# An attention and RWKV decoder layer on one core: ranking by eight-largest operations, the compression's first rows and weights loaded one stage earlier, and the dilated cache's loads issued from three queues

## What is computed

```
P = h @ w_in                               # one projection, split among all branches
A = native sparse attention:
      compressed blocks: each block of 32 cached rows (stride 16) of keys and of values goes through
                         hid = gelu((rows + phi_pe) @ phi_w1); row = hid @ phi_w2
      selected blocks:   score of each of 65 blocks of 64 tokens from the compressed weights, plus a bonus
                         for forced blocks; the 16 highest (ties: lower index first) are attended in full
      window:            the last 512 tokens
B = RWKV-7 time mixing (a recurrence)
C = dilated window attention, 3 groups of 4 heads with (window, step) = (128,1), (512,4), (2048,16)
m = sum of the three branches, gated;  x = LayerNorm(alpha * x + gate * (m @ w_o))
x = LayerNorm(alpha * x + gate * SwiGLU(x))
```

## Time and profile before

| | us |
|---|---|
| median of 3 runs | 2117.22 |
| runs | 2113.62 to 2125.13 |
| the profiled execution | 2136.6 |
| its span, first to last instruction | 2134.8 |
| TensorE busy | 1816.2 (85%) |
| VectorE busy | 1066.3 (50%) |
| ScalarE busy | 667.8 (31%) |
| GpSimd busy | 201.3 (9%) |
| mean granted TensorE clock | 0.919 of full speed |

### The profile page before, as it was taken

One profiled execution on the slowest core, in us unless ns is written; L12 is line 12 of the kernel. 1 busy time (PEld: TensorE's weight loads), 2 busy tenths in 40 slices (PEclk: granted clock), 3 DMA queues, 4 the chain that ended last, 5 costly groups with the idle time before them and its releaser, 6 DMA issues. The chain is left out here.

```text
span 2134.8 us, 39918 instructions
## 1 busy us (share of the span) xinstructions
PE 1816.2 (85%) x16882; PEld 1633.4 (77%) x16882; DVE 1066.3 (50%) x1722; ACT 667.8 (31%) x1306; POOL 201.3 (9%) x245
## 2 busy tenths in 40 slices
PE   3898788887989869998877999656599799999996
PEld 1898678776888868897875667434499699999996
DVE  3114656666655325685865545592276443333333
ACT  1225333332212212332324766323342422221122
POOL 0000000000001114221100001244100000000000
PEclk7999899998999988999987999778799899999998
DMA  6546754342536758766656252657363133232221
GB/s 245 152 123 199 208 154 142 112 152 90 172 111 202 225 163 273 194 204 174 147 145 259 88 154 66 199 175 260 119 225 112 30 99 90 81 90 82 83 72 43
DMA packets 334304, 315.61 MB, mean 148 GB/s; under 512 B 119533, under 2 KB 292133, under 8 KB 328622
## 3 DMA queue, kind: packets, MB, share of 16 engines
q1 hardware_dynamic: 311406, 195.30, 30.8%
q0 software_dynamic: 22720, 117.75, 16.6%
HBM read 285.51 MB, written 79.71 MB: 171 GB/s over the span
## 5 line engine op out<-in xcount | busy, mean ns | idle before, releaser
L308 PE MATMUL inp_acc<-hh,inp_wh 128*128 128x272 f32 (+1 forms) x1072 | 344.3, 321 | 43.8 <-DVE inp_wl L280 24.2
L308 PE MATMUL inp_acc<-hh,inp_wl 128*128 128x272 f32 (+1 forms) x1072 | 318.2, 297 | 0.0
L308 PE MATMUL inp_acc<-hl,inp_wh 128*128 128x272 f32 (+1 forms) x1072 | 317.8, 296 | 0.0
L308 PEld LDWEIGHTS inp_acc<-hh,inp_wh 128*128 128x128 f32 (+1 forms) x1072 | 209.2, 195 | 66.4 <-issue 33.3
L308 PEld LDWEIGHTS inp_acc<-hl,inp_wh 128*128 128x128 f32 (+1 forms) x1072 | 210.1, 196 | 3.5 <-issue 3.2
L280 DVE TENSOR_TENSOR inp_wl<-inp_w,inp_wh 128x1024 fp32r<-128x1024 f32 (+1 forms) x67 | 81.2, 1212 | 261.0 <-ACT inp_wh L460 260.5
L308 PEld LDWEIGHTS inp_acc<-hh,inp_wl 128*128 128x128 f32 (+1 forms) x1072 | 209.5, 195 | 0.5
L280 DVE TENSOR_TENSOR fwl<-fw,fwh 128x1024 fp32r<-128x1024 f32 (+1 forms) x68 | 81.1, 1193 | 169.6 <-ACT fwh L2077 166.3
L2077 ACT ACTIVATE fwh<-fw 128x1024 fp32r<-128x1024 f32 (+1 forms) x65 | 67.1, 1034 | 296.6 <-PE ffn_acc L289 296.6
L289 PE MATMUL ffn_acc<-ffn_hh,fwh 128*128 128x272 f32 x704 | 146.6, 290 | 12.0 <-DVE ffn_hl L280 11.0
L1363 PE MATMUL cmp_pH<-cmp_RTh,cmp_w1h 128*128 128x256 f32 (+1 forms) x512 | 151.5, 296 | 0.0
(11 more groups left out here) (520 smaller groups left out, 3852.1 us busy)
## 6 DMA issues: line engine op xcount, KB each, us to landing
inp_w<-in_w_in_dram SPq DMA_DIRECT2D x66, 512.0 KB, 6.8
out_dram<-in_cache_dil_dram POOLq DMA_DIRECT2D x64, 511.0 KB, 5.4
fw<-in_w_ffn_dram SPq DMA_DIRECT2D x60, 512.0 KB, 3.8
shared<-in_cache_dil_dram SPq DMA_DIRECT2D x192, 86.0 KB
PT<-inp_o SPq DMA_DIRECT2D x58, 272.0 KB, 3.0
front<-in_w_ada_dram SPq DMA_DIRECT2D x12, 1024.0 KB, 5.7
ada_wada<-in_w_ada_dram SPq DMA_DIRECT2D x8, 1024.0 KB, 9.0
out_dram<-in_cache_dil_dram POOLq DMA_DIRECT2D x16, 508.0 KB, 8.3
```

Source lines behind the costliest of these rows:

```text
L308: i = pe.matmul(out, l, r, start=(first and n == 0), stop=(last and n == 2))
```

## The change

It has four parts.

1. **Memory.** `oaT`, `ocT`, `idx`, `front` and a new small `pages` are allocated ahead of the projection stage; many of the mixer's buffers now are parts of `oaT`, `ocT` and `front`.
2. **First rows and weights.** SyncE loads the page table at the head of the projection stage, VectorE makes the indices there (`index_vector`). At the mixer's due number `c_at(7, 4)` = 103.3, once `final` and `osp` say that the memory is free, SyncE loads w1 and GpSimd gathers work 0. In the compression stage `turn(0)` is TensorE's first work, w1 is split in two halves (`halved`) around low(0), and the one-column products stand behind hidden(0). w2 is loaded by GpSimd at work 4.
3. **Dilated loads.** SyncE loads heads 0 and 1, ScalarE head 2, GpSimd head 3 (`others`), each with its own waits for `used`; GpSimd's loads of pieces 0 and 1 stand ahead of the gather of work 1. Head 3 has semaphores of its own (`third`).
4. **Ranking.** For each half f: the eight largest scores, these replaced by a large negative number, the next eight, replaced too; a compare then gives the mask from what was replaced. `tri` isn't loaded. Values 0 to 2 wait for nothing, value 3 for `cpv`; GpSimd's order is keys 1 to 5, values 0 to 3, keys 6 to 9, values 4 and 5, keys 10 to 13, values 6 and 7, keys 14 and 15, the other values. The mask follows each chunk at once, and the exponentials of the first half stand one unit earlier.

The diff, cut to its core:

```diff
-        self.pbt, self.xm = sb("pbt", [P, 14, P + 1]), sb("xm", [P, 14, P])
+        flat = lambda name: m[name][:, :, :].rearrange("p c t -> p (c t)")
+        self.pbt = flat("oaT")[:, 0:14 * (P + 1)].rearrange("p (n t) -> p n t", n=14)
+        front = lambda at, n: m["front"][:, at:at + n * P].rearrange("p (n t) -> p n t", n=n)
+        self.xm = front(0, 14)
...
+        yield self.c_at(NCH - 1, 4)
+        sp.wait_ge(self.final, 4)
+        sp.wait_ge(self.osp, NCH)
+        sp.dma_start(m["front"][:, 0:4096].rearrange("p (v c h) -> p v c h", v=2, c=16),
+                     a["phi_w1"][0].rearrange("v l d h -> v (l d) h").rearrange("v (c p) h -> p v c h", p=P)).then_inc(m["first_weights"], 16)
...
+        yield self.c_at(NCH - 1, 4)
+        pool.wait_ge(self.m["index_built"], 4)
+        pool.wait_ge(self.final, 4)
+        pool.wait_ge(self.osp, NCH)
+        src = self.a["cache_nsa_cmp"][0].rearrange("n v g (c l) d -> (n v g c) (l d)", l=16)
+        for h in range(2):
+            pool.indirect_dma_start(
+                out=self.m["front"][:, 4096 + h * 1024:4096 + (h + 1) * 1024], out_offset=None, in_=src,
+                in_offset=bass.IndirectOffsetOnAxis(ap=self.m["idx"][:, 0, h:h + 1], axis=0),
+            ).then_inc(self.m["first_rows"], 16)
...
+    def index_vector(self, dve):
+        m = self.m
+        pages, lane = m["pages"][:, 0:2 * DB], m["pages"][:, 2 * DB:2 * DB + 1]
+        c = Chain(dve, self.ich)
+        yield PROLOGUE
+        dve.wait_ge(m["pages_in"], 32)
+        c(dve.tensor_scalar(pages, pages, 32.0, None, ALU.mult))
+        c(dve.tensor_tensor(pages, pages, lane.to_broadcast([P, 2 * DB]), ALU.add))
+        for i in range(4):
+            dve.tensor_scalar(m["idx"][:, i, :], pages, float(8 * i), None, ALU.add).then_inc(m["index_built"], 1)
...
+            if w == 0:
+                continue
+            yield -4.5 + w if w < self.NR else min(w, 14 + w / 2) - 6.5
             if w >= self.NR:
                 pool.wait_ge(self.turned, self.read(w - self.NR))
             elif w == 4:
-                pool.wait_ge(self.wfree, 3)
+                pool.dma_start(self.w2[:, :, :], a["phi_w2"][0].rearrange("v h d -> h v d")).then_inc(self.outer, 16)
+                pool.wait_ge(self.wfree, 1)
...
+            if c in (0, 2) and i < 4:
+                pe.wait_ge(self.halved, c // 2 + 1)
...
         yield -3
-        pe.wait_ge(self.loaded, 80)
+        turn(0)
+        yield -1
+        pe.wait_ge(self.loaded, 16)
         pe.transpose(pK[:, 0, 0:32], self.per[:, :], m["ident"][0:32, 0:32]).then_inc(self.pet, 1)
-        pe.wait_ge(self.pek, 1)
-        for v in range(2):
-            for c in range(16):
-                i = pe.matmul(pH[:, 0, v:v + 1], self.w1[:, v, c, :], self.peT[:, v * 16 + c:v * 16 + c + 1], start=(c == 0), stop=(c == 15))
-        i.then_inc(self.hcd, 1)
-        yield -1
-        turn(0)
-        pe.wait_ge(self.wfree, 3)
...
+            if i == 0:
+                pe.wait_ge(self.pek, 1)
+                pe.wait_ge(m["first_weights"], 16)
+                for v in range(2):
+                    for c in range(16):
+                        x = pe.matmul(pK[:, 0, 64 + v:65 + v], self.w1[:, v, c, :], self.peT[:, v * 16 + c:v * 16 + c + 1], start=(c == 0), stop=(c == 15))
+                x.then_inc(self.hcd, 1)
...
+        def weights(v):
+            ch(split_high(dve, self.w1h[:, v], self.w1[:, v]))
+            split_low(dve, self.w1l[:, v], self.w1[:, v], self.w1h[:, v]).then_inc(self.halved, 1)
...
+        dve.wait_ge(self.pet, 1)
+        dve.tensor_copy(self.peT[:, :], self.pK[:, 0, 0:32]).then_inc(self.pek, 1)
+        weights(1)
+        dve.wait_ge(self.hcd, 1)
+        dve.tensor_copy(self.hc[:, :], self.pK[:, 0, 64:66]).then_inc(self.hck, 1)
+        dve.wait_ge(self.halved, 2)
+        dve.sem_inc(self.wfree, 1)
...
+        a, done = self.a, (self.third if heads == (3,) else self.here)[i % self.NB]
+        for h in heads:
...
+    def others(self, eng, head, late):
+
+        for i in range(len(self.order)):
+            if i < self.NB:
+                yield -5 + i if head == 3 else -0.95 if i == 0 else 0.7 * i
+            else:
+                yield self.at(i - self.NB, 1 + late)
+                eng.wait_ge(self.used, i - self.NB + 1)
+            self.load(eng, i, (head,))
...
-            dve.wait_ge(self.here[i % self.NB], self.arrived(i))
+            dve.wait_ge(self.here[i % self.NB], 3 * self.arrived(i))
+            dve.wait_ge(self.third[i % self.NB], self.arrived(i))
...
-                cmp.pool(pool)
+                weave(cmp.pool(pool), dil.others(pool, 3, 0))
...
-                weave(cmp.scalar(act), dil.scalar(act))
+                weave(cmp.scalar(act), dil.scalar(act), dil.others(act, 2, 0.15))
...
-                    if j < 4:
-                        pool.wait_ge(rk, 2)
+                    if j < 3:
+                        pass
+                    elif j == 3:
...
-                for i in range(1, 10):
+                for i in range(1, 6):
                     keys(i)
                 for j in range(4):
                     values(j)
-                keys(10)
-                keys(11)
+                for i in range(6, 10):
+                    keys(i)
                 values(4)
                 values(5)
-                for i in range(12, 16):
+                for i in range(10, 14):
                     keys(i)
-                for j in (6, 7, 8, 9, 10, 11, 14, 15, 12, 13):
+                values(6)
+                values(7)
+                keys(14)
+                keys(15)
+                for j in (8, 9, 10, 11, 14, 15, 12, 13):
...
-                            yield (43 + q if f == 0 else 74 + 0.5 * q) + 0.2
+                            yield (42 + q if f == 0 else 74 + 0.5 * q) + 0.2
...
-                    dve.wait_ge(lt, 16)
-                    at = 9.2
+                    yield 9.2
                     for f in range(2):
-                        for j0, j1 in HALVES:
-                            B = [P, j1 - j0, NBLK]
-                            x = cmpb[:, 0:j1 - j0, :]
-                            si = score[:, f, :].unsqueeze(1).to_broadcast(B)
-                            sj = score[:, f, j0:j1].unsqueeze(2).to_broadcast(B)
-                            yield at
-                            c(dve.tensor_tensor(x, si, sj, ALU.is_equal))
-                            yield at + 1.2
-                            c(dve.tensor_tensor(x, x, tri[:, j0:j1, :], ALU.mult))
-                            yield at + 2.4
-                            c(dve.tensor_reduce(rank[:, f, j0:j1], x, AX, ALU.add))
-                            yield at + 3.6
-                            c(dve.tensor_tensor(x, si, sj, ALU.is_gt))
-                            yield at + 4.8
-                            c(dve.tensor_reduce(selb[:, f, j0:j1], x, AX, ALU.add))
-                            at += 6
-                        c(dve.tensor_tensor(rank[:, f, :], rank[:, f, :], selb[:, f, :], ALU.add))
-                        c(dve.tensor_scalar(selb[:, f, :], rank[:, f, :], TOPN - 0.5, -BIG, ALU.is_gt, ALU.mult))
+                        c(dve.max(top[:, f, 0, :], score[:, f, :]))
+                        c(dve.match_replace(rest[:, f, :], top[:, f, 0, :], score[:, f, :], -BIG))
+                        c(dve.max(top[:, f, 1, :], rest[:, f, :]))
+                        c(dve.match_replace(rest[:, f, :], top[:, f, 1, :], rest[:, f, :], -BIG))
+                        c(dve.tensor_scalar(selb[:, f, :], rest[:, f, :], -0.5 * BIG, -BIG, ALU.is_gt, ALU.mult))
                         dve.sem_inc(rk, 1)
...
-                            yield max(8 + 4 * (8 * f + w) + 4.6, 34.2 + 0.7 * w)
+                            yield 8 + 4 * (8 * f + w) + 4.6
```

98 lines of the change are left out of this document (40 added, 58 removed).

## The result

The changed kernel takes 2092.75 us (median of 3 runs, 2091.27 to 2094.47) against 2117.22: a ratio of 0.9889, with a 95% interval of 0.9862 to 0.9915. That is 24.5 us faster where 80 were forecast, and above the range's upper end of 2088.

The account below looks back on a forecast made before the run. The prediction held that TensorE fully bounds none of the three stages, each having a wait that ends last. Its terms, +5 - 11 - 40 - 34 = -80, took 2117.2 us to 2037, range 1998 to 2088.

Parts of the forecast that it names:

- Laying buffers over others, making indices early: Memory and projection prologue: only addresses change, and six small index operations move where VectorE is a quarter busy; 0 us.
- Projection, +5 forecast: Projection stage: w1 and two gathers come in, lengthening TensorE's stall behind a late tile; +5 us, bounds 0 and 12.
- Start, -11 forecast: Compression start: rows, index and w1 ready at the barrier bring hidden 1 earlier; -11 us, ends -20 and 0.
- Rival B: Waits move: late work 1 gather, keys 14 and 15 behind values, projection stall of 12; about 2080 us, chance 0.12.
- Dilated loads, -40 forecast: Compression's steady part: three issuing queues recover most of 55 us lost; -40 us, range -55 to -10.
- ScalarE is only 94 of 317 us busy: Steady part: ScalarE's 4.4 to 5.5 us of issues per piece mostly hide in 4.88 us of waiting per step.
- Rival D: Steady part: ScalarE's dilated issues block casts and gelu, 8 us a piece, +120 us; about 2157 us, chance 0.06.
- SyncE ceases to be late: Steady part: SyncE needs 9 to 11 us for its half of a piece where the work gives 14.1 us.
- Rival A: Steady part: the DMA engines bound it, not the issuer, so its gain is 0; about 2077 us, chance 0.22.
- the 55 us called lost: Steady part: time above undisturbed steps, 309.7 us against 250.9 plus some 4, free if nothing else replaces it.
- my 254.9: Steady part without losses: 32 steps of 7.84 us, 250.9, plus some 4 for four wider steps.
- Sample attention, -34 forecast: Sample attention: cheaper ranking and keys 10 issued earlier bring the last score group forward; -34 us, ends -48 and -15.

Follow-up runs that it names:

- e4: The changed kernel with w1's load issued behind the last w_in tile: 2084.3 us.
- b_again: The kernel before, profiled a second time with no edit: span 2119.5 us.
- e2: The changed kernel with all four heads of the dilated loads on SyncE's queue again: 2097.5 us.
- e7: The changed kernel with head 2 on SyncE, w1 behind the last w_in tile, one-column products before turn 1, work 1's gather before GpSimd's first dilated loads: 2044.8 us.
- e3: The changed kernel with head 2 of the dilated loads on SyncE instead of ScalarE: 2067.7 us.
- e15: e7 with dilated loads of groups 1 and 2 reading rows side by side, so the dilated branch computes from other data: 2036.4 us.

## Why the prediction was wrong

**Laying buffers over others, making indices early**: nothing, as said.

**Projection, +5 forecast, +11.8 measured.** The mechanism was named, the next tile behind w1 in the queue, and the measured value is the upper bound. I chose by the amount of free DMA time over 98 us. The failing step: the load is not spread over the stage. The store behind w1 waits until w1 has moved, 14.48 us, and with it the one tile that TensorE needs next. e4 shows that the amount was indeed free and the place was not.

**Start, -11 forecast.** Step 1's first product stood 47.7 us behind the projection's last one (836.8 - 789.1), where it was 51.1 before and 45.7 in b_again: no gain that can be told from zero. The order of events was right; the gather of work 1 was forecast 17.7 us behind the projection's end and came at 21.9, and the one-column products took 11.7, near their upper end. Rival B had this piece. e2 shows that the eight loads ahead of the gather cost 7 us, e7 that products and gap fit beside each other.

**Dilated loads, -40 forecast, -10 to -14 measured.** From step 1's first product to the last gelu it is 291.7 us; before it was 301.7, in b_again 305.4. The step that failed is the overlap on ScalarE: "ScalarE is only 94 of 317 us busy, and each step leaves it 4.88 us of waiting, so mostly hidden". The price of the issues was right: forecast 4.4 to 5.5 us a piece, measured 4.9 (73.8 us for 15 pieces), though one set of four took 14.72. What wasn't hidden is the two together, a wait on `used` and then the issues in one block, 7 to 20 us ahead of a gelu: ScalarE did no work for 92.9 us ahead of eight gelus, of which some 37 us are waiting for `used` by the rows of its queue, and VectorE waited 49.1 us for its casts instead of 6.1. Without ScalarE's share the part is 18 us shorter (273.4 in e3) and the kernel 25 us faster. The 4.88 us of idle time in a step can't take up a block of twice its length. Rival D named that mechanism and set it at 8 us a piece with 0.06; it cost 25 us in all (e3), 1.7 us for each of 15 pieces on the mean, not enough to turn the sign.

The second step that failed is "SyncE ceases to be late". With 12 loads a piece SyncE took 1.74 us for each in e3, and VectorE still waited 28.9 us. Rival A was half right: with 256 B rows and gathers in flight an issue waits, whoever makes it, and the sum over queues didn't rise (24 loads in 41.7 us on SyncE and 8 on GpSimd, against 32 in 35.58 on one). It was wrong that helpers give nothing: GpSimd's gave 30. By the Trainium skill, "DMA: Bandwidth & Descriptors", section "Issuing engines are not separate DMA queues", helpers save issuing time alone; the measured pair (5 us for two helpers, 30 for one) shows that what they cost at their own engine has to be counted beside it. The size was off too: of the 55 us called lost, e15 without waits on loads has 264.8 us against my 254.9, so 10 us of it didn't go even there.

**Sample attention, -34 forecast, -22 measured** against b_again (-42 against the first profile). The price of the new operations was right (2.5 us forecast, 2.6 by their rows). So was the stage's own course: the last score group was forecast 135 us behind the stage's start and stands at 130, the stage was forecast at 168 us and took 159.7. What was wrong is what it was taken from, a stage of 201.8 us that is 182.0 in the other execution. Against that one the end was held back by keys 14 and 15 behind values 6 and 7, 11 us, which the prediction had as a piece of rival B and priced into no likelier case; without them it is -33. That 168 and 159.7 lie near each other is in part luck: the 20 us too much in the base and the 11 us that were missed point opposite ways.

**The sum.** Against b_again: +11.8 (its projection ended 3.5 us later than in the first profile, so +8.2 there), +2.0, -13.7 and -22.3, and -3.1 in the stretch that nothing touches, make -28.9, and the two spans differ by 28.6; the medians say -24.5. Against the first profile, from which the forecast was made, the terms missed by +6.8, +7.6, +30.0 and -8.1, 36 us in all; the other 19 of the 56 us between 2037 and 2092.75 are that this profile's gain of 44 us is 24.5 by the medians. Of rival B's three pieces the projection's and the start's came true in full and the sample's in part, and with them D's ScalarE; the forecast had these as alternatives at 0.12 and 0.06, when each was a defect in a stage of its own that nothing in the other stages spoke against.
